# Scores of the local attention, issued in pairs of heads from different halves of the array's rows

## The reference

```python
A_HEADS = 6; A_KV = 2; A_DH = 64; WINDOW = 128

def swa_branch(q, k, v, sinks):
    G = A_HEADS // A_KV
    qb = q.reshape(B, nb, WINDOW, A_KV, G, A_DH)
    ...
    kk = jnp.concatenate([jnp.concatenate([pad, kh[:, :-1]], 1), kh], 2)   # block before, this block
    scores = jnp.einsum('bnqkgd,bnskd->bnkgqs', qb, kk).astype(jnp.float32) * (A_DH ** -0.5)
    ...
    scores = jnp.where(valid[None, :, None, None], scores + alibi[None, None], -jnp.inf)
    probs = jax.nn.softmax(jnp.concatenate([scores, sink], axis=-1), axis=-1)[..., :-1]
    out = jnp.einsum('bnkgqs,bnskd->bnqkgd', probs.astype(v.dtype), vv)
```

## Time and profile before

| | us |
|---|---|
| median of 3 runs | 2555.04 (2552.13 to 2558.71) |
| the profiled execution | 2557.66 |
| its span, first to last instruction | 2556.0 |
| stage 2 in it | 962 to 1929 |
| PE busy, whole span | 2254.4 (88%) |
| DVE busy, whole span | 1525.8 (60%) |

### The profile page before, as it was taken

The page is one execution under the profiler, slowest core; times in us unless marked ns, Lnnn a source line. Parts: engine busy times, 40 slices in busy tenths (PEclk is TensorE's granted clock), DMA queues, the critical chain, the costliest instruction groups (busy, mean ns, idle before and its releaser), DMA issues. The chain is left out here.

```text
span 2556.0 us, 51831 instructions
## 1 busy us (share of the span) xinstructions
PE 2254.4 (88%) x20878; PEld 1700.4 (67%) x21010; DVE 1525.8 (60%) x2366; ACT 1056.0 (41%) x2294; POOL 570.3 (22%) x540
## 2 busy tenths in 40 slices
PE   1799999999999971799999999999983889889887
PEld 1576666766667631798899998899971555655554
DVE  6544434444344426476666676666665787878775
ACT  2433334333333323233332333332333776868664
POOL 0600000100001002224333324333332232323221
PEclk9899999999999985899999999999985999999999
DMA  9200000000000008101000001000107201121101
GB/s 399 98 18 18 26 18 18 26 18 22 22 18 26 18 19 325 39 26 35 27 27 26 29 24 35 28 27 26 29 16 255 66 25 58 33 67 50 58 33 41
DMA packets 82207, 138.56 MB, mean 54 GB/s; under 512 B 42432, under 2 KB 63040, under 8 KB 77904
## 3 DMA queue, kind: packets, MB, share of 16 engines
q1 hardware_dynamic: 82000, 135.50, 15.4%
HBM read 104.01 MB, written 31.46 MB: 53 GB/s over the span
## 5 line engine op out<-in xcount | busy, mean ns | idle before, releaser
L1298 PE MATMUL m_bank<-m_arena,m_w_hi 128*128 128x128 bf16 (+1 forms) x2560 | 453.0, 224 | 22.8 <-DVE m_w_lo L1270 22.4
L1299 PE MATMUL m_bank<-m_arena,m_w_hi 128*128 128x128 bf16 (+1 forms) x2560 | 452.5, 221 | 0.0
L1300 PE MATMUL m_bank<-m_arena,m_w_lo 128*128 128x128 bf16 (+1 forms) x2560 | 452.3, 222 | 0.0
L1298 PEld LDWEIGHTS m_bank<-m_arena,m_w_hi 128*128 128x128 bf16 (+1 forms) x2560 | 252.7, 99 | 28.7 <-DVE m_w_lo L1270 22.8
L1299 PEld LDWEIGHTS m_bank<-m_arena,m_w_hi 128*128 128x128 bf16 (+1 forms) x2560 | 257.2, 100 | 0.3
L1300 PEld LDWEIGHTS m_bank<-m_arena,m_w_lo 128*128 128x128 bf16 (+1 forms) x2560 | 251.3, 98 | 0.0
L1693 POOL TENSOR_TENSOR s_hi<-s_sp,s_cols 128x512 bf16<-128x512 f32 x144 | 152.8, 1061 | 428.4 <-DVE s_sp L1824 243.2
L217 POOL TENSOR_TENSOR g_stage<-g_stage,g_nh_row 128x1024 f32<-128x1024 f32 x16 | 52.3, 3268 | 751.2 <-DVE g_stage L486 751.2
L552 PE MATMUL g_bank<-g_h_hi,g_wi_hi 128*128 128x128 bf16 (+1 forms) x1152 | 197.0, 220 | 18.9 <-DVE g_wi_lo L504 18.7
L553 PE MATMUL g_bank<-g_h_lo,g_wi_hi 128*128 128x128 bf16 (+1 forms) x1152 | 196.6, 220 | 0.0
L554 PE MATMUL g_bank<-g_h_hi,g_wi_lo 128*128 128x128 bf16 (+1 forms) x1152 | 196.6, 220 | 0.0
(11 more groups left out here) (360 smaller groups left out, 5665.4 us busy)
## 6 DMA issues: line engine op xcount, KB each, us to landing
m_arena<-in_w_in_dram SPq DMA_DIRECT2D x8, 1618.0 KB, 8.8
g_stage<-in_gla_w_in_dram SPq DMA_DIRECT2D x8, 1544.0 KB, 12.4
g_stage<-in_ada_w_dram SPq DMA_DIRECT2D x8, 1536.0 KB, 11.2
g_xs<-in_x_dram SPq DMA_DIRECT2D x16, 512.0 KB, 3.5
x<-g_stage SPq DMA_DIRECT2D x16, 512.0 KB, 2.7
m_arena<-in_w_mod_dram SPq DMA_DIRECT2D x8, 1024.0 KB, 7.1
m_arena<-x SPq DMA_DIRECT2D x16, 512.0 KB, 3.8
s_xr<-x SPq DMA_DIRECT2D x16, 512.0 KB, 4.0
```

What stands on the lines that cost most here:

```text
L1298: pe.matmul(out, l_hi, r_hi, start=(k == 0), stop=False)
L1299: pe.matmul(out, l_hi, r_lo, start=False, stop=False)
L1300: ins = pe.matmul(out, l_lo, r_hi, start=False, stop=(k == n - 1))
```

## The change

PE issues the same 12 scores per tile with the same operands and results, in another order. Before, the heads came as 0, 1, 2, 4, 5, 3, each with both of its key blocks in succession. Now they come as three pairs (0, 3), (1, 4), (2, 5), and within a pair, for each key block, the low-half head and then the high-half head. The semaphore is turned round: head 3 now writes bank B5 first, and the pair that holds head 2 waits for it.

```diff
-                for head in (0, 1, 2, 4, 5, 3):
-                    if head == 3:
-
-                        pe.wait_ge(s["head_2_scored"], i + 1)
+                for pair in ((0, 3), (1, 4), (2, 5)):
+                    if 2 in pair:
+                        pe.wait_ge(s["head_3_scored"], i + 1)
                     for half in range(1 if first else 0, 2):
-                        slot = par if half else 1 - par
-                        ...
-                        ins = pe.matmul((B3, B5, B6)[head // 2][:, at:at + T], aq[ps, j, :], ak[ps, slot, :],
-                                        start=True, stop=True)
-                    if head == 2:
-                        ins.then_inc(s["head_2_scored"], 1)
+                        for head in pair:
+                            slot = par if half else 1 - par
+                            ...
+                            ins = pe.matmul((B3, B5, B6)[head // 2][:, at:at + T], aq[ps, j, :], ak[ps, slot, :],
+                                            start=True, stop=True)
+                    if 3 in pair:
+                        ins.then_inc(s["head_3_scored"], 1)
                 ins.then_inc(s["scores_done"], 1)
```

More of the change, by code:

```diff
@@ L785, in mix_phase @@
                  "rows_done silu_one silu_rec silu_done sqk_split ym_out ya_out sq_out sk_out sv_out sz_out dve_pre act_pre dve_link act_link "
-                 "head_2_scored").split()
+                 "head_3_scored").split()
         sem = phase_semaphores(nc, ctx, "m_")
@@ L1452, in tile @@
                     pe.wait_ge(s["hf_done"], 2 * (i + 2))
-                for head in (0, 1, 2, 4, 5, 3):
-                    if head == 3:
-                        pe.wait_ge(s["head_2_scored"], i + 1)
+                for pair in ((0, 3), (1, 4), (2, 5)):
+                    if 2 in pair:
+                        pe.wait_ge(s["head_3_scored"], i + 1)
                     for half in range(1 if first else 0, 2):
-                        slot = par if half else 1 - par
-                        g, j = head // AG, head % AG
-                        ps = slice(g * AD, (g + 1) * AD)
-                        at = (head % 2) * 2 * T + half * T
-                        ins = pe.matmul((B3, B5, B6)[head // 2][:, at:at + T], aq[ps, j, :], ak[ps, slot, :],
-                                        start=True, stop=True)
-                    if head == 2:
-                        ins.then_inc(s["head_2_scored"], 1)
+                        for head in pair:
+                            slot = par if half else 1 - par
+                            g, j = head // AG, head % AG
+                            ps = slice(g * AD, (g + 1) * AD)
+                            at = (head % 2) * 2 * T + half * T
+                            ins = pe.matmul((B3, B5, B6)[head // 2][:, at:at + T], aq[ps, j, :], ak[ps, slot, :],
+                                            start=True, stop=True)
+                    if 3 in pair:
+                        ins.then_inc(s["head_3_scored"], 1)
                 ins.then_inc(s["scores_done"], 1)
```

## The result

The changed kernel takes 2583.07 us (median of 6 runs, 2575.36 to 2586.99), the kernel before 2554.43 us on the same chip (6 runs, 2547.96 to 2558.71). The ratio is 1.0111, with a 95% interval of 1.0091 to 1.0131. That is 28.6 us more where 0.8 us less was forecast, and outside the range of 2549 to 2563 us. The profiled execution took 2584.63 us, with a span of 2582.7.

A forecast was written before the change was run, and what follows sets the result against it. The prediction took a chain through DVE, POOL and ACT to the wait at L1354 to set each tile. Its terms, 15 x 0 - 0.8 = -0.8 us, took the median from 2555.04 to 2554.3 us, range 2549 to 2563.

The forecast's parts named there:

- The clock: PE's granted clock in stage 2: no net change in falls to 1.2 GHz, each costing 1.6 us; called the least certain term.
- More falls of the clock: Rival: longer idle time before L1354 adds a fall in tiles without one, 2564.6 us; two per tile, +34 us; chance 8%.
- The scores: L1462 on PE: pairs of records overlap, so the scores take 1.59 us per tile instead of 2.60.
- The turned semaphore: Wait of pair (2, 5) for head 3's second block: covered by pair (1, 4); 0.1 to 0.3 us per tile if not.
- The gate columns: L1298 on PE: starts 0.65 us earlier; the other 0.36 us become a wait for DVE's L1136.
- The wait at L1354: PE's wait for ACT's L1010 before probabilities times values: grows from 1.06 to 1.65 us per tile.
- the 1.01 us per tile: Time the paired scores save on PE in each tile, with no gain in the 15 passages between tiles.
- the sum: Total over stage 2: 15 x 0 - 0.8 = -0.8 us, giving a median of 2554.3 us.
- The tail: Last tile to the end of the stage: DVE's 0.77 us wait for the scores goes, gain 0.8 us.
- a stall at the passages between the halves: Rival: ten more passages between row halves in the scores drain the array, 2.4 us per tile, 2592 us; chance 3%.
- PE was not the bound: Rival denied here: PE bounds the stage 2 tiles, so 16 us come back and the median is 2539; chance 3%.

## Why the prediction was wrong

The step that failed is the one headed "The clock". It put the net change at nothing, and reasoned that a fall before L1354 would take the place of the one at 1440.6. Its rival, "More falls of the clock", named the right mechanism with a chance of 8% and priced it at 10.4 us, or at 34 us with two falls in each tile; the tiles from first to last scores gave 24.9. Two things in it were wrong:

- *Instead of, or as well.* The falls at L1354 came beside those behind L1402, both in one tile (1265.9 and 1279.5), in 6 of the 8 tiles of the 13 that have a fall, and in place of them in only 2. The single tile of 57.04 us in the earlier trace rows, with a fall at each of the two places, was the pattern to come, and I set it aside as one in 14.
- *The length of a fall.* I priced each at 1.6 us, from falls that end in dense products. One that begins early in L1354 lasts 6.8 us and costs 3.3 us. In the changed kernel and in the runs with few scores and with L1402 moved alone (on either kernel), each fall that began within 1.8 us of the start of L1354 lasted 6.8 us, and each that began later in it 3.4 us; both kinds occur in each of these four traces. In the earlier trace rows the fall at 1211.9 began 2.5 us behind the start of L1354, so it didn't show this. A reading that fits, and that no run tests by itself, is that the narrow matmuls that are left take nearly twice as long at half the clock (L1354 4.55 us instead of 2.89) and so keep PE's work thin.

Against the rival I held that 13 tiles had the same idle time of 1.06 us and no fall. That was an argument about 1.06 us, and the change made it 1.6. The experiments show only short falls at 0.95 us and mostly long ones at 1.59, and at 1.06 us a small shift of other work was enough for some long ones (the run with L1402 moved alone). The rows I had showed that the fall followed idle time and narrow matmuls; the right reading was that more idle time there is a cost of its own. What stays open is why a fall follows L1354 in one tile and not in the next: in the changed kernel the wait is 1.59 to 1.60 us in all 13 tiles, and 5 of them have no fall at all.

The other steps held. The scores take 1.61 us (1.59 forecast), by the overlap read from the earlier trace rows. The turned semaphore shows no wait. The gate columns wait 0.28 us for L1136 (0.36 forecast). The wait at L1354 is 1.59 to 1.60 us (1.65 forecast), and a tile without a fall is still 53.77 us: the 1.01 us per tile came to nothing, as the sum had it, since the chain through DVE, POOL and ACT sets the tile. The tail gave 0.9 us (0.8 forecast). Of the rivals, a stall at the passages between the halves didn't occur, and PE was not the bound, which the moved copies then changed.

The difference of the spans in stage 3 (+4.2 us) isn't explained by an experiment. There, behind the stage's start, the changed kernel's trace has 11 falls of 3.4 us and that of the kernel before 7; whether that is chance isn't shown. The six runs of either kernel spread by 11 to 12 us.

## What to carry to other kernels

Work saved on an engine that then waits is not free of charge where the engine is PE: the saved time turns into idle time at the wait, and if narrow matmuls follow, the granted clock may fall and take back more than was saved. Before shortening PE's work, find the wait that sets the tile and cut that first, here by moving three copies ahead of an unrelated wait; the same shortening was then a gain. Price a fall of the clock by where it begins (here 1.6 or 3.3 us), and look for every stretch of thin work: here mending one of the two moved the falls to the other.

## What the runs showed of the hardware

- Work that nobody reads can make a kernel faster: 7 matmuls per tile in the idle time took 2583 us to 2547 us.
- Thin work lowers the granted clock even where PE shows no idle time: behind L1395 to L1402 it is 0.50 from 1440.6 to 1444.0, and PE was busy for all of the 3.50 us before that:

```profile
1437.10:1440.60 3.50, 3.50 (x40) 2.89 (x38) 2.91 (x4) 2.37 (x9) 0.16 (x1) 0.99 0.15 56
```

- The falls of the clock tie themselves to the tiles. In the kernel before one comes in every second tile and costs 1.6 us, in the changed kernel 8 of the 13 tiles have falls (4 have one of 6.8 us and one of 3.4, 2 have two of 3.4, 2 have one of 6.8), and the other 5 tiles last 53.77 us.
- Float32 matmuls over 64 rows in different halves of the array do run side by side: 24 records take 1.61 us against 2.60. Their order in the program need not be strictly alternating for it: at the one passage of the old order 10 records already stood where 6 stand elsewhere.
